# Reordering the opening of the two seven-product stages of a two-block transformer kernel

## The chip, the cores and the metric

One core of a Trainium2 chip. The metric is device time in microseconds (us); lower is better. Engines are named as in the profile: PE (TensorE matmul), PEld (its weight load), DVE (VectorE), ACT (ScalarE), POOL (GpSimd), SP (SyncE, which issues most loads).

## The reference, cut to what matters

All data are float32, 1024 tokens of width 1024. The first block (short convolution, stick-breaking attention) is untouched by the change. In the second block two wide projections matter here, each on a modulated norm `h` of the residual stream:

```python
h = _rmsnorm(x, norm1_g[l]) * (1.0 + scale1) + shift1
proj = h @ w_in[l]                    # 4352 columns: q, k, v of two attentions, two gates
...
h2 = _rmsnorm(x, norm2_g[l]) * (1.0 + scale2) + shift2
u = h2 @ w_up[l]                      # 2 x 2816 columns
a, g = jnp.split(u, 2, axis=-1)
a = ap[:, 0:s] * conv_w[0] + ap[:, 1:s + 1] * conv_w[1] + ap[:, 2:s + 2] * conv_w[2] + conv_b
x = x + gate2 * ((jax.nn.gelu(a, approximate=False) * g) @ w_down)
```

## The kernel before, in words

Channels lie on the 128 partitions, tokens along the free axis, in two halves of 512. Every fp32 product is made of three products of split operands (high by high, low by high, high by low), each part a rounded copy or the rest that it leaves. A high part is an ACT copy, a low part a DVE subtraction that waits for that copy.

Both projections run as two stages of one shape, called here the w_in stage (`U_IN2`, 15 blocks) and the w_up stage (`U_FFN`, 20 blocks). A stage opens with a `quad` (L1804): four ordinary units of 128 output columns, `q` to `q+3`, computed in the order (first pair, tokens 0 to 511), (second pair, both halves), (first pair, tokens 512 to 1023). Then come blocks `i` of 256 output columns, each by seven products (a Strassen-Winograd scheme, 2 by 2 by 2) of 12 matmuls of 128x128 by 128x512, in the order P1, P2, P6, P5, P7, P4, P3 (`sevens`, L1848). A block needs

- four weight sums on POOL (`weight_sums`, L1731), seven high parts on ACT (`weight_high`, L2274) and seven low parts on DVE (`weight_low`, L2966);
- three copies out of PSUM on ACT in the middle of the block (`snap`, L2305): snap 0 after P1, on which P6 waits; snap 1 after P6, on which P7 waits; snap 2 after P7, on which the first of four DVE `block_sum` (L2994) waits, and P3 waits on that one;
- for block 0 only, the sums of the tokens (`token_sums` L2984, 4 DVE subtractions for each of four chunks), their high parts on ACT (`token_high` L2296) and their low parts on DVE (`token_low` L2976), 16 of each.

What the blocks give is used further on. In the w_in stage `in2_copy` (L2325) takes a pair of the quad out of PSUM, `in2_use` (L2334) and `in2_low` (L3012) split a finished block of 128 columns into staging tiles, and `in2_store` (L2358) stores it by two DMAs of 512 KB, issued by ACT; the next use of a staging row waits until the store has landed. In the w_up stage each chunk `f` of 128 channels goes through a chain that changes engine at every step, for each half of the tokens: `first_tap` (ACT), `other_taps` (DVE, two instructions), `gelu` (ACT), the product with the gate (DVE; `first_product` for the two chunks of the quad, `gated` for others), `z_high` (ACT), `z_low` (DVE), and then `z_store` (two DMAs issued by ACT for both halves). One tile `yt` with two halves serves all chunks, so the next chunk's first tap in a half waits for the `z_low` of the chunk before it in that half.

Every engine executes its queue strictly in the order in which the program text issues it; nothing is reordered by a planner. The order inside a stage is written out by hand: `in2_act` (L2377) and the lines from L2544 for ACT, `in2_dve` (L3023) and the lines from L3152 for DVE. A semaphore wait holds back all that stands behind it on the same engine.

## Time and profile before

| what | value |
|---|---|
| median of 3 runs | 2747.52 us (2745.22 to 2749.78) |
| profiled execution, its own time | 2748.31 us |
| its span, first to last instruction | 2746.5 us |
| PE busy | 2600.3 us, 95% of the span |
| DVE, ACT, POOL busy | 56%, 40%, 31% |
| w_in stage, blocks 0 and 1 | from 1341.29 to 1387.04 us of the span |
| w_up stage, blocks 0 and 1 | from 2076.26 to 2136.50 us of the span |

The two openings are the stretches that the change is about; the rows below show them. In a timeline the idle time of an engine before a row stands in brackets, with the instruction that ended it.

### The profile page before, as it was taken

Reading aid. Unit: us, or ns where it says so; the run is one execution under the profiler, and the core shown is the slowest. Engines: PE = TensorE matmul, PEld = TensorE weight load, DVE = VectorE, ACT = ScalarE, POOL = GpSimd, SP = SyncE. Lnnn points to the kernel's source line nnn. Section 1 sums busy time; section 2 is a strip of 40 time slices with the busy share of each in tenths; the row PEclk is TensorE's granted clock in tenths of the full one; section 3 lists DMA queues with packets and bytes.
Section 4 is the critical chain, followed back from the end, with each engine's and each line's share of the span. In section 5 each row is a group of like instructions: output and inputs, shape, how many; then the busy total and the mean of one; then the engine's idle time right before and its main releaser. Section 6 shows DMA issues by size and latency. Waiting matters only on the chain.

```text
span 2746.5 us, 34710 instructions
## 1 busy us (share of the span) xinstructions
PE 2600.3 (95%) x12391; PEld 2162.4 (79%) x12391; DVE 1535.8 (56%) x2083; ACT 1109.9 (40%) x1865; POOL 855.9 (31%) x627
## 2 busy tenths in 40 slices
PE   6899999999899999999899998789997999999998
PEld 4788888788788799987688878668775888887887
DVE  5666665630324466657854437766578777771112
ACT  5201012511410688856543437661255555551000
POOL 2133331022233566620222220333101322325664
PEclk8999999999999999999999999999998999999999
DMA  6445443353365544435253346414242333339833
GB/s 226 127 125 149 131 149 98 89 191 113 124 211 163 130 108 108 108 127 160 88 183 122 108 138 171 159 33 169 79 136 91 100 117 108 108 109 304 285 93 122
DMA packets 377272, 374.81 MB, mean 136 GB/s; under 512 B 36323, under 2 KB 284556, under 8 KB 376972
## 3 DMA queue, kind: packets, MB, share of 16 engines
q1 hardware_dynamic: 346844, 303.91, 37.3%
q10 hardware_dynamic: 30256, 68.69, 6.7%
q8 instruction: 99, 1.62, 0.3%
q14 instruction: 73, 0.60, 0.1%
HBM read 286.55 MB, written 85.98 MB: 136 GB/s over the span
## 4 chain that ended last, share of the span: by engine, by line
PE 75%; DVE 12%; ACT 5%; DMA 3%; issue 2%; SPq 1%; POOL 1%; ACTq 0%; DVEq 0%; POOLq 0%
PE PS L1769 28%; PE PS L1857 20%; PE PS L1926 8%; PE PS L809 5%; PE PS L787 2%; PE PS L1816 1%; PE PS L1997 1%; DMA mod_raw<-in_w_ada 1%; PE PS L773 1%; PE PS L772 1%; DVE opBf L2991 1%; PE PS L1971 1%; ACT opA L2145 1%; PE PS L1839 1%; ACT opBf L2141 1%
## 5 line engine op out<-in xcount | busy, mean ns | idle before, releaser
L1769 PE MATMUL PS<-opA,w_hi 128*128 128x512 f32 x2176 | 680.3, 392 | 3.0 <-POOL w_lo L1575 3.0
L1769 PEld LDWEIGHTS PS<-opA,w_hi 128*128 128x128 f32 x2176 | 411.2, 189 | 89.0 <-POOL w_lo L1575 3.4
L1769 PE MATMUL PS<-opA,w_lo 128*128 128x512 f32 x1088 | 425.4, 391 | 0.0
L1570 POOL CAST w_hi<-w_raw 128x1024 fp32r<-128x1024 f32 (+1 forms) x117 | 121.3, 1037 | 795.7 <-PE PS L1769 467.3
L1857 PE MATMUL PS<-opB,Xr 128*128 128x512 f32 x1120 | 312.0, 396 | 17.4 <-ACT M L2321 17.4
L1575 POOL TENSOR_TENSOR w_lo<-w_raw,w_hi 128x1024 fp32r<-128x1024 f32 (+1 forms) x118 | 284.9, 2414 | 36.2 <-ACT w_hi L2200 26.8
L1857 PE MATMUL PS<-opA,Xr 128*128 128x512 f32 x980 | 277.3, 393 | 6.3 <-DVE M L3008 3.0
L1857 PEld LDWEIGHTS PS<-opB,Xr 128*128 128x128 f32 x1120 | 214.7, 192 | 64.1 <-ACT M L2321 18.6
L2656 DVE SCALAR_TENSOR_TENSOR M<-mod_raw,small,M 128x512 f32<-128x512 f32 x168 | 169.0, 1006 | 165.5 <-DMA mod_raw<-in_w_ada 88.6
L1769 PEld LDWEIGHTS PS<-opA,w_lo 128*128 128x128 f32 x1088 | 205.8, 189 | 42.7 <-issue 0.2
L1857 PEld LDWEIGHTS PS<-opA,Xr 128*128 128x128 f32 x980 | 183.0, 189 | 50.3 <-ACT M L2321 8.4
L2934 DVE SCALAR_TENSOR_TENSOR X<-PS,mod,X 128x512 f32<-128x512 f32 x64 | 48.1, 751 | 297.8 <-PE PS L1926 207.8
L1857 PE MATMUL PS<-opA,w_first 128*128 128x512 f32 x840 | 197.6, 391 | 5.6 <-ACT M L2331 5.6
L1857 PEld LDWEIGHTS PS<-opA,w_first 128*128 128x128 f32 x840 | 158.7, 189 | 39.0 <-ACT M L2331 6.0
L1743 POOL TENSOR_TENSOR X<-w_raw 128x512 f32<-128x512 f32 x36 | 48.5, 1347 | 379.6 <-DVE xn L2729 228.1
L1769 PE MATMUL PS<-opB,w_hi 128*128 128x512 f32 x512 | 159.9, 392 | 2.4 <-DVE opB L2922 1.4
L1128 DVE TENSOR_TENSOR_SCAN M<-PS,beta 128x896 f32<-128x896 f32 (+7 forms) x86 | 116.4, 1360 | 69.7 <-ACT PS L1004 61.8
L3008 DVE TENSOR_TENSOR M<-M,PS 128x512 f32<-128x512 f32 x140 | 96.3, 688 | 101.0 <-ACT M L2321 66.0
L2972 DVE TENSOR_TENSOR Xr<-X,Xr 128x512 fp32r<-128x512 f32 x140 | 117.0, 836 | 63.3 <-ACT Xr L2293 55.2
L1926 PE MATMUL PS<-opA,w_hi 128*128 128x512 f32 x480 | 149.2, 389 | 0.0
L2216 ACT ACTIVATE squares<-X 128x512 f32<-128x512 f32 x48 | 30.4, 633 | 232.6 <-DVE X L2934 229.2
L2321 ACT ACTIVATE M<-PS 128x512 f32<-128x512 f32 x105 | 62.8, 598 | 151.6 <-PE PS L1857 128.2
(266 smaller groups left out, 4794.9 us busy)
## 6 DMA issues: line engine op xcount, KB each, us to landing
mod_raw<-in_w_ada SPq DMA_DIRECT2D x96, 256.0 KB, 3.0
z_dram<-opB ACTq DMA_DIRECT2D x44, 512.0 KB, 3.9
w_raw<-in_a_w_in SPq DMA_DIRECT2D x32, 512.0 KB, 4.8
hin<-q_dram SPq DMA_DIRECT2D x64, 256.0 KB, 6.0
w_raw<-in_w_down SPq DMA_DIRECT2D x32, 512.0 KB, 3.9
opA<-z_dram SPq DMA_DIRECT2D x60, 256.0 KB, 5.3
mod_raw<-in_b_mod_w SPq DMA_DIRECT2D x48, 256.0 KB, 2.9
X<-x_dram SPq DMA_DIRECT2D x24, 512.0 KB, 6.9
```

The source lines that it names most:

```text
L787: ins = pe.transpose(PS[:, 4 + c % 2, (kb - NQ * p) * P:(kb - NQ * p + 1) * P], beta[n % BETAS][:, kb * P:(kb + 1) * P], ident[:])
L809: ins = pe.matmul(PS[:, o, q0 + cols_of.start:q0 + 2 * P], head_v[s][:, kb * P:(kb + 1) * P], a_T[i // 2][kb // NQ][:, kb % NQ, cols_of], ...
L1128: dve.tensor_tensor_scan(rest[n % FACTORS][:, 0:w][:, ::-1], stick_z(n)[:, ::-1], beta[n % BETAS][:, 0:w][:, ::-1], 1.0, ALU.mult, ALU.byp ...
L1570: pool.tensor_copy(hi, raw).then_inc(pool_done, 1)
L1575: pool.tensor_tensor(lo, raw, hi.bitcast(F32), ALU.subtract).then_inc(pool_done, 1)
L1769: ins = pe.matmul(ps, w[:, k0 + k, :], rhs(part, k0 + k), start=(k == 0 and n == 0), stop=(k == chunks - 1 and n == 2))
L1857: ins = pe.matmul(PS[:, seven_bank(i, which), :], seven_weight(q, i, which, w)[:, c * P:(c + 1) * P], token_part(which, part, c), start=(s ...
L1926: ins = pe.matmul(PS[:, down_bank(hf, n), :], w[:, s, k, :], z_operand(hf, g, part, k), start=(g == 0 and k == 0 and m == 0), stop=(g == 2 ...
L2321: act.activation(block_tile(q, i, 1)[:, 0:HALF] if n == 2 else M[1][:, n * HALF:(n + 1) * HALF], PS[:, seven_bank(i, P1), :], ACT.Copy).th ...
L2656: dve.scalar_tensor_tensor(out=acc, in0=mod_raw[:, n % 2, :], scalar=c, in1=acc, op0=ALU.mult, op1=ALU.add).then_inc(dve_done, 1)
L2972: dve.tensor_tensor(seven_weight(q, i, which, 1), seven_source(i, which), seven_weight(q, i, which, 0).bitcast(F32), ALU.subtract).then_in ...
L3008: dve.tensor_tensor(tile[:, hf * HALF:(hf + 1) * HALF], former, PS[:, seven_bank(i, which), :], ALU.add).then_inc(dve_done, 1)
```

## The change

On the order of work, in both stages:

- ACT's high parts: tokens of chunks 0 and 1, then the weights of P6, P5, P1 and P2, then the copies of the quad's second pair, and only then tokens of chunks 2 and 3 and the weights of P7 and P3. DVE follows with its low parts (P1 and P2 before the token sums of chunks 2 and 3).
- To free the P5 half of the PSUM early, the second of these copies goes aside: unit `q+3` is copied into a free half of `X` (chunks 6 and 7) by `in2_copy` in the w_in stage, and by the new `first_gates` in the w_up stage, where it is the gate of chunk 0.
- POOL's weight sums of block 1 wait for the last `token_low` of block 0.
- The high parts of the tokens of P7 and P4 wait for a new signal of PE in the middle of the quad's last quarter (`b12_read`), not for the end of unit `q+1`.
- Block 0's last two block sums move ahead of block 1's last weights on DVE; ACT's uses and stores of the quad's units take other places between block 1's weight copies.
- In the w_up stage chunk 0 is no longer finished first. Its copy goes into `M[4]` (`first_tile`), and its chain runs by halves: tokens 512 to 1023 inside block 1, tokens 0 to 511 from the end of block 1 into block 2. `copied_product` multiplies with the gate that was copied aside. Snap 0 of block 1 moves ahead of `gelu(2, 0)`.

The diff, cut to its core:

```diff
+        def z_former(f):
+            return {0: 2, 1: None, 2: None, 4: 0}.get(f, f - 2)
+        def gelu_former(f, hf):
+            return {1: None, 2: 1, 0: 2 if hf else 3, 4: 3 if hf else 0, 3: 0 if hf else 2}.get(f, f - 1)
+        def in2_halves(i, row):
+            return X[:, 6:8, HALF:T] if (i, row) == (-2, 1) else halves_of(block_tile(U_IN2, i, row)[:])
...
                     pool.wait_ge(seven_in[i % 2], at("seven_in", q, i))
+                    if i == 1:
+                        pool.wait_ge(dve_done, at("token_lo", q, P4, QK - 1))
...
+                        if (first, hf, k) == (0, 1, QK - 1):
+                            ins.then_inc(pe_done, 1)
+                            step(pe_done, "b12_read", u)
...
                 if which in (P7, P4):
-                    act.wait_ge(pe_done, at("unit", q + 1, 1))
+                    act.wait_ge(pe_done, at("b12_read", q))
...
                 weight_high(q, 0, P4)
-                token_high(q, P5, 0)
-                token_high(q, P6, 0)
+                for c in range(2):
+                    token_high(q, P5, c)
+                    token_high(q, P6, c)
                 weight_high(q, 0, P6)
                 weight_high(q, 0, P5)
-                token_high(q, P5, 1)
-                token_high(q, P6, 1)
-                weight_high(q, 0, P7)
-                weight_high(q, 0, P3)
-                for c in (2, 3):
-                    token_high(q, P5, c)
-                    token_high(q, P6, c)
                 weight_high(q, 0, P1)
                 weight_high(q, 0, P2)
                 for row in range(2):
                     in2_copy(-2, row)
+                for c in (2, 3):
+                    token_high(q, P5, c)
+                    token_high(q, P6, c)
+                weight_high(q, 0, P7)
+                weight_high(q, 0, P3)
                 for c in range(QK):
                     token_high(q, P7, c)
                 snap(q, 0, 0)
                 for c in range(QK):
                     token_high(q, P4, c)
+                weight_high(q, 1, P1)
+                snap(q, 0, 1)
+                weight_high(q, 1, P2)
                 for row in range(2):
                     in2_copy(-1, row)
-                snap(q, 0, 1)
-                for row in range(2):
-                    in2_use(-2, row)
-                weight_high(q, 1, P1)
-                weight_high(q, 1, P2)
-                for row in range(2):
-                    in2_store(-2, row)
+                in2_use(-2, 0)
                 snap(q, 0, 2)
+                in2_use(-2, 1)
                 weight_high(q, 1, P6)
                 weight_high(q, 1, P5)
                 for row in range(2):
+                    in2_store(-2, row)
+                weight_high(q, 1, P7)
+                for row in range(2):
                     in2_use(-1, row)
-                weight_high(q, 1, P7)
                 weight_high(q, 1, P4)
...
```

The same diff, ACT's order in the w_up stage from block 0's snap 2 on:

```diff
             for hf in range(2):
                 z_high(1, hf)
-            first_tap(2, 0)
             weight_high(q, 1, P7)
             weight_high(q, 1, P4)
+            first_tap(2, 0)
             z_store(1)
+            snap(q, 1, 0)
             gelu(2, 0)
             z_high(2, 0)
             first_tap(2, 1)
             for i in range(1, SEVENS[q]):
                 f = i + 2
-                snap(q, i, 0)
+                if i > 1:
+                    snap(q, i, 0)
                 weight_high(q, i + 1, P1)
                 weight_high(q, i, P3)
                 gelu(f - 1, 1)
                 z_high(f - 1, 1)
+                if i == 2:
+                    gelu(0, 0)
                 weight_high(q, i + 1, P2)
+                if i == 2:
+                    z_high(0, 0)
                 first_tap(f, 0)
                 z_store(f - 1)
+                if i == 2:
+                    z_store(0)
                 snap(q, i, 1)
                 weight_high(q, i + 1, P6)
                 gelu(f, 0)
+                if i == 1:
+                    first_tap(0, 1)
                 weight_high(q, i + 1, P5)
+                if i == 1:
+                    gelu(0, 1)
                 snap(q, i, 2)
                 weight_high(q, i + 1, P7)
                 weight_high(q, i + 1, P4)
                 z_high(f, 0)
+                if i == 1:
+                    z_high(0, 1)
                 first_tap(f, 1)
+                if i == 1:
+                    first_tap(0, 0)
...
```

DVE's order in the w_in stage behind the `token_low` instructions:

```diff
-                for row in range(2):
-                    in2_low(-2, row)
+                weight_low(q, 1, P1)
                 block_sum(q, 0, 1, 1)
+                weight_low(q, 1, P2)
+                in2_low(-2, 0)
                 block_sum(q, 0, 0, 0)
-                for which in (P1, P2, P6, P5):
-                    weight_low(q, 1, which)
+                weight_low(q, 1, P6)
+                weight_low(q, 1, P5)
+                in2_low(-2, 1)
+                block_sum(q, 0, 0, 1)
+                block_sum(q, 0, 1, 0)
+                weight_low(q, 1, P7)
                 for row in range(2):
                     in2_low(-1, row)
+                weight_low(q, 1, P4)
...
```

DVE's order in the blocks of the w_up stage from block 1 on:

```diff
+                other_taps(f - 1, 1)
+                weight_low(q, i + 1, P1)
+                weight_low(q, i, P3)
+                gated(f - 1, 1)
+                if i == 2:
+                    other_taps(0, 0)
+                block_sum(q, i, 0, 0)
+                z_low(f - 1, 1)
+                if i == 2:
+                    copied_product(0)
+                weight_low(q, i + 1, P2)
+                if i == 2:
+                    z_low(0, 0)
+                other_taps(f, 0)
+                weight_low(q, i + 1, P6)
+                weight_low(q, i + 1, P5)
+                if i == 1:
+                    other_taps(0, 1)
+                block_sum(q, i, 1, 1)
                 weight_low(q, i + 1, P7)
                 block_sum(q, i, 1, 0)
                 gated(f, 0)
+                if i == 1:
+                    copied_product(1)
                 weight_low(q, i + 1, P4)
                 z_low(f, 0)
+                if i == 1:
+                    z_low(0, 1)
                 block_sum(q, i, 0, 1)
```

## Rows read from the trace of the kernel before

**Rows 1.** The page's first part: busy time of each engine

```profile
PE 2600.3 (95%) x12391; PEld 2162.4 (79%) x12391; DVE 1535.8 (56%) x2083; ACT 1109.9 (40%) x1865; POOL 855.9 (31%) x627
```

**Rows 2.** Timeline of PE, w_in stage: start, duration, line, count, [idle before]

```profile
1324.68 11.04 PE L1816 MATMUL PS<-opA,opB 128*128 128x512 f32 x48
1341.29 7.16 PE L1857 MATMUL PS<-opA,w_first 128*128 128x512 f32 x24 [5.57 <-ACT M L2331]
...
1371.69 7.35 PE L1857 MATMUL PS<-opB,Xr 128*128 128x512 f32 x24 [2.34 <-ACT M L2321]
...
1387.04 5.60 PE L1857 MATMUL PS<-opA,w_first 128*128 128x512 f32 x24
```

**Rows 3.** Timeline of PE, w_up stage

```profile
2065.38 11.04 PE L1816 MATMUL PS<-opA,opB 128*128 128x512 f32 x48
2076.26 5.60 PE L1857 MATMUL PS<-opA,w_first 128*128 128x512 f32 x24
2085.59 7.08 PE L1857 MATMUL PS<-opB,Xr 128*128 128x512 f32 x24 [3.72 <-ACT M L2321]
...
2102.98 5.60 PE L1857 MATMUL PS<-opA,w_first 128*128 128x512 f32 x24
2119.91 8.59 PE L1857 MATMUL PS<-opB,Xr 128*128 128x512 f32 x24 [11.32 <-ACT M L2321]
...
2136.50 5.60 PE L1857 MATMUL PS<-opA,w_first 128*128 128x512 f32 x24
...
2155.54 5.60 PE L1857 MATMUL PS<-opA,w_first 128*128 128x512 f32 x24
```

**Rows 4.** Timeline of DVE, w_in stage

```profile
1323.01 2.87 DVE L2991 TENSOR_TENSOR opBf<-opBf 128x512 f32<-128x512 f32 x4
...
1332.91 5.76 DVE L2991 TENSOR_TENSOR opBf<-opBf 128x512 f32<-128x512 f32 x4
1339.38 1.49 DVE L2972 TENSOR_TENSOR w_first<-w_raw,w_first 128x512 fp32r<-128x512 f32 x2 [0.71 <-ACT w_first L2293]
1340.97 6.27 DVE L2980 TENSOR_TENSOR opB<-opBf,opB 128x512 fp32r<-128x512 f32 x8
...
1353.72 2.67 DVE L3019 SCALAR_TENSOR_TENSOR opB<-M,small,opB 128x1024 fp32r<-128x1024 f32 x2
...
1370.52 0.69 DVE L3008 TENSOR_TENSOR M<-M,PS 128x512 f32<-128x512 f32 x1
```

**Rows 5.** Timeline of ACT and its DMA queue, w_in stage

```profile
1355.77 3.51 ACTq L2367 DMA_DIRECT2D q_dram<-opB  x4
...
1363.09 1.15 ACT L2355 ACTIVATE opB<-M,small 128x1024 fp32r<-128x1024 f32 x1 [0.29 <-DMA q_dram<-opB]
...
1371.04 0.60 ACT L2321 ACTIVATE M<-PS 128x512 f32<-128x512 f32 x1 [5.31 <-DVE Xr L2972]
```

**Rows 6.** DMA issues, 1340 to 1430 us: count, size, median us to landing

```profile
q_dram<-opB ACTq DMA_DIRECT2D x16, 512.0 KB, 3.9
```

**Rows 7.** Timeline of POOL, w_in stage

```profile
1370.52 1.27 POOL L1743 TENSOR_TENSOR X<-w_raw 128x512 f32<-128x512 f32 x1 [2.01 <-DVE Xr L2972]
```

**Rows 8.** Timeline of ACT, w_up stage, block 2

```profile
2139.41 0.60 ACT L2321 ACTIVATE M<-PS 128x512 f32<-128x512 f32 x1 [0.45 <-PE PS L1857]
2144.81 1.19 ACTq L2529 DMA_DIRECT2D z_dram<-opB  x2
2146.13 0.60 ACT L2321 ACTIVATE M<-PS 128x512 f32<-128x512 f32 x1 [0.71 <-DVE w_first L2972]
```

**Rows 9.** Timeline of DVE, w_up stage, blocks 1 and 2

```profile
2108.31 2.37 DVE L3129 TENSOR_TENSOR opB<-yt,opB 128x512 fp32r<-128x512 f32 x2
2110.78 2.35 DVE L3140 SCALAR_TENSOR_TENSOR yt<-M,cols,yt 128x511 f32<-128x511 f32 x2
```

**Rows 10.** Windows: length, then busy us of PE, PEld, DVE, ACT, POOL; granted clock

```profile
2103.00:2136.50 33.50, 22.18 (x86) 17.74 (x84) 25.85 (x34) 15.60 (x24) 10.25 (x7) 0.80 0.28 95
...
2155.50:2174.60 19.10, 19.10 (x86) 15.79 (x86) 14.52 (x20) 10.23 (x17) 5.70 (x4) 1.00 0.35 111
```

More of the change, by code:

```diff
@@ L2330, in in2_copy @@
                 act.wait_ge(act_done, now(act_done))
-                act.activation(block_tile(U_IN2, i, row)[:], banks(bank(u, 0)), ACT.Copy).then_inc(act_done, 1)
+                if (i, row) == (-2, 1):
+                    act.wait_ge(x_half[1], at("x_half", U_IN2, 1))
+                act.activation(in2_halves(i, row), PS[:, bank(u, 0):bank(u, 0) + 2, :], ACT.Copy).then_inc(act_done, 1)
                 step(act_done, "in2_copy", u)
@@ L2354, in in2_use @@
                 else:
-                    act.activation(in2_stage(row, 0), halves_of(tile[:]), ACT.Copy, scale=in2_scale(in2_place(u))).then_inc(act_done, 1)
+                    act.activation(in2_stage(row, 0), in2_halves(i, row), ACT.Copy, scale=in2_scale(in2_place(u))).then_inc(act_done, 1)
                     step(act_done, "in2_used", u)
@@ L2498, in first_copies, with first_gates @@
                     act.wait_ge(pe_done, at("unit", u, 1))
-                    act.wait_ge(dve_done, at("fconv", f - 1, 1) if f else at("lo", "n2", 15))
+                    act.wait_ge(dve_done, at("lo", "n2", 15))
                     act.wait_ge(act_done, now(act_done))
-                    act.activation(M[0][:, hf * HALF:(hf + 1) * HALF], PS[:, bank(u, hf), :], ACT.Copy).then_inc(act_done, 1)
+                    act.activation(first_tile(f)[:, hf * HALF:(hf + 1) * HALF], PS[:, bank(u, hf), :], ACT.Copy).then_inc(act_done, 1)
                     step(act_done, "fa", f, hf)
                 names[("free", u)] = names[("fa", f, 1)]
+            def first_gates(u):
+                for hf in range(2):
+                    act.wait_ge(pe_done, at("unit", u, 1))
+                    act.wait_ge(x_half[1], at("x_half", U_FFN, 1))
+                    act.wait_ge(dve_done, at("lo", "n2", 15))
+                    act.wait_ge(act_done, now(act_done))
+                    act.activation(first_gate(hf), PS[:, bank(u, hf), :], ACT.Copy).then_inc(act_done, 1)
+                    step(act_done, "first_gate", hf)
             def gelu(f, hf):
@@ L2545, in _ @@
             weight_high(q, 0, P4)
-            token_high(q, P5, 0)
-            token_high(q, P6, 0)
+            for c in range(2):
+                token_high(q, P5, c)
+                token_high(q, P6, c)
             weight_high(q, 0, P6)
             weight_high(q, 0, P5)
-            token_high(q, P5, 1)
-            token_high(q, P6, 1)
-            weight_high(q, 0, P7)
-            weight_high(q, 0, P3)
+            weight_high(q, 0, P1)
+            weight_high(q, 0, P2)
+            first_copies(*CLASSIC[0])
+            first_gates(U_FFN + 3)
             for c in (2, 3):
@@ L2556, in _ @@
                 token_high(q, P6, c)
-            weight_high(q, 0, P1)
-            weight_high(q, 0, P2)
-            first_copies(*CLASSIC[0])
-            for hf in range(2):
-                first_tap(0, hf)
-            for hf in range(2):
-                gelu(0, hf)
+            weight_high(q, 0, P7)
+            weight_high(q, 0, P3)
             for c in range(QK):
@@ L2569, in _ @@
             first_copies(*CLASSIC[1])
-            snap(q, 0, 1)
-            for hf in range(2):
-                z_high(0, hf)
-            weight_high(q, 1, P1)
-            weight_high(q, 1, P2)
             for hf in range(2):
                 first_tap(1, hf)
-            z_store(0)
+            weight_high(q, 1, P1)
+            snap(q, 0, 1)
+            weight_high(q, 1, P2)
             snap(q, 0, 2)
@@ L2998, in block_sum @@
                 dve.wait_ge(act_done, at("snap", q, i, n))
-                if q == U_IN2:
+                if q == U_IN2 and (i, row) != (0, 1):
                     u = in2_unit(i - 2, row)
@@ L3123, in first_product, with copied_product @@
                 names[("free", u + 1)] = names[("fz", f, 1)]
+            def copied_product(hf):
+                dve.wait_ge(act_done, at("fg", 0, hf))
+                dve.wait_ge(act_done, at("first_gate", hf))
+                dve.wait_ge(dve_done, now(dve_done))
+                dve.tensor_tensor(yt[:, hf, :], yt[:, hf, :], first_gate(hf), ALU.mult).then_inc(dve_done, 1)
+                step(dve_done, "fz", 0, hf)
             def z_low(f, hf):
@@ L3157, in _ @@
             weight_low(q, 0, P5)
+            weight_low(q, 0, P1)
+            weight_low(q, 0, P2)
             token_sums(q, 2)
+            token_sums(q, 3)
             weight_low(q, 0, P7)
             weight_low(q, 0, P3)
-            token_sums(q, 3)
-            weight_low(q, 0, P1)
-            weight_low(q, 0, P2)
-            for hf in range(2):
-                other_taps(0, hf)
-            for c in range(QK):
-                token_low(q, P6, c)
-            for c in range(QK):
-                token_low(q, P5, c)
-            first_product(*CLASSIC[0])
-            for c in range(QK):
-                token_low(q, P7, c)
-            for c in range(QK):
-                token_low(q, P4, c)
-            for hf in range(2):
-                z_low(0, hf)
+            for which in (P6, P5, P7, P4):
+                for c in range(QK):
+                    token_low(q, which, c)
             weight_low(q, 1, P1)
+            weight_low(q, 1, P2)
             block_sum(q, 0, 1, 1)
@@ L3181, in _ @@
             block_sum(q, 0, 0, 0)
-            weight_low(q, 1, P2)
             first_product(*CLASSIC[1])
```

77 lines of the change are left out of this document (39 added, 38 removed).

## Prediction, made before the changed kernel had run

> **What bounds the kernel now.** I read the busy shares first: PE works 95% of the span, the next engine 56% [rows 1], so outside its gaps the time is PE's. Then PE's timeline in the two openings. A settled block of 84 matmuls takes 2155.54 - 2136.50 = 19.04 us [rows 3], 0.2267 us a matmul, 2.72 a product. In the w_in stage the quad's last 48 matmuls start at 1324.68 and could end at 1335.56; two blocks at full rate would bring block 2 to 1373.64, and it starts at 1387.04 [rows 2]: 13.4 us lost. In the w_up stage they could end at 2076.26, block 2 could start at 2114.34, and starts at 2136.50 [rows 3]: 22.2 us lost. Together 35.6 us, 1.3%, is the most that this change can give. The brackets name what PE waited for: in the w_in stage the copy of the quad (5.57 us, L2331) and snap 0 of block 1 (2.34); in the w_up stage snap 0 of blocks 0 and 1 (3.72, 11.32). All are ACT instructions at the end of a long queue, so the question is not whether PE waits but what stands ahead of each snap.
>
> The clock belongs to it. Behind the 11.32 us gap the granted clock of the window is 0.80 [rows 10], and the remaining 60 matmuls of the block take 2136.50 - 2119.91 = 16.59 us for 13.60: 3.0 us for the lower level. Behind 2.34 us of idle they take 15.35 (1.75 lost), behind 3.72 us 24 matmuls take 7.08 for 5.60 (1.5 lost) [rows 2, 3].
>
> I now walk the new queues by durations of rows. One 128x512 DVE subtraction takes 0.69 and follows the next at 0.72 to 0.80 us; 16 token lows take 2 x 6.27; `in2_low` 1.33 [rows 4]. Where POOL's sums run beside them, the four token sums of 2.87 take 5.76 [rows 4] and two z_low or two taps 2.4 instead of 1.5 [rows 9]: about 0.95 us of delay for each POOL sum. A block sum, which reads PSUM, keeps its 0.69 beside a running POOL sum [rows 4, 7].
>
> **W_in stage, block 0: the gain.** Copies of the quad now come before the last tokens, and POOL's four sums of block 1 no longer lie on the token sums, which take back their 2.87. From the second group of sums (end 1325.88): four weight lows behind their copies to 1329.74, eight token sums to 1335.5, two weight lows behind their ACT copies to 1337.8, then 16 lows at 0.784 to 1350.6, where before they ended at 1353.6. ACT has both copies done at 1331.1, so P1 starts at 1335.56 without the 5.57 us gap and its slow matmuls. The lows come each 3.14 us for a product of 2.72, so PE trails them: P6 1341.1, P5 1344.3, P7 1347.5, P4 1350.7, P3 1353.4, end 1356.1, against 1363.75: 7.6 us ahead. The early signal for P7 and P4 buys nothing here: their ACT copies are reached at 1337, after unit `q+1` anyway, and their lows wait in DVE's queue.
>
> **W_in stage, block 1: where it goes.** P6 of block 1 needs snap 0, and ACT reaches it only behind both stores of the units `q` and `q+1`. The chain ahead of it, from 1350.6: DVE does four weight lows, two block sums and two `in2_low` (7.5 us), and POOL's sums, moved to just here by the added wait, delay the ones that read SBUF twice by 4 x 0.95. So the second `in2_low` ends at 1361.9; before, both were done at 1356.39 [rows 4]. That is 5.5 us later, since its ACT copy now stands behind snap 2 and its DVE part behind two weight lows that wait for POOL. Then: store 1.2 (two DMAs), landing 3.9 us after the second issue at 1362.6 [rows 6], next use 1.15, `in2_low` 1.3 to 1.6, store 1.2, snap 0.6. Snap 0 ends at 1371.1 to 1371.9; I take 1371.5, against 1371.64 before [rows 5]. PE is idle from 1361.5 to 1371.5, ten microseconds; the nearest row is the 11.32 us gap, so the rest of the block takes 16.6 instead of 15.35, and block 2 starts at 1388.1 against 1387.04: **+1.1 us**. Bounds: with no POOL delay, and the clock loss of rows 2, -4; with the landing of rows 5 (the staging row was waited for until 1363.09, 3.8 us after the last issue had ended at 1359.28) and more delay by POOL, +3.
>
> **W_up stage, blocks 0 and 1.** The same walk: lows of P6 to P4 end at 2079.2, 2082.3, 2085.5 and 2088.7, because chunk 0's taps, gelus and product no longer stand among them. P6 starts at 2081.7, P7 at 2087.4 (ACT's second copies and first taps stand ahead of snap 1), and block 0 ends at 2095.6 against 2102.98: -7.4. P1 and P2 of block 1 end at 2101.0. Ahead of its snap 0 now stand chunk 1's whole chain, two weight copies, `first_tap(2, 0)` and `z_store(1)`: taps of chunk 1 beside POOL's sums to 2097.7, gelu, product to 2100.1, two weight lows, two block sums, `z_low` beside POOL 2103.4 to 2105.8 [rows 9], tap, store, snap 0 ended at 2107.8. P6 starts there, 12.1 us earlier than before. But the edit that moves snap 0 forward leaves `gelu(2, 0)`, `z_high(2, 0)` and `first_tap(2, 1)` between snap 0 and snap 1. From 2107.8: taps end 2110.3, product, z_high and tap 2113.5, two weight copies, gelu(2, 1) 2115.7, product, z_high 2118.1, tap and store, snap 1 ended at 2121.5. In a settled block it starts 6.72 us after snap 0 [rows 8]; here 13.7. PE has finished P5 at about 2115 and stands for 6 us; the clock falls again (1.6 us). Then `first_tap(0, 1)`, its taps and `gelu(0, 1)` stand ahead of snap 2, which P3 waits for by way of the block sum: it starts at 2130.2, 1.6 us late. Block 2 starts at 2133.0 against 2136.50: **-3.5 us**, bounds -6 and -1.
>
> **W_up stage, block 2.** In a settled block the queues have room as a whole: of 19.1 us DVE works 14.5, ACT 10.2 [rows 10]. But PE needs snap 1 10.9 us after the block's start, and it is there (2146.73 for 2147.38) 0.65 us before. That is all the cover there is, and everything inserted ahead of snap 1 beyond it is PE's time. Late already at the start: DVE's `copied_product(1)` and `z_low(0, 1)` and ACT's `z_high(0, 1)` and `first_tap(0, 0)` stand between block 1's end and snap 0, which starts at 2138.9, 5.9 us into the block instead of 2.9; P6 waits 1.1 us. Ahead of snap 1 come, in turns between engines, taps of (0, 0) on DVE to +5.4 us after snap 0 (+6.7 if POOL's sum goes first), gelu, block sum, z_low, `copied_product` +7.8, z_high +8.5, z_low +9.4, tap +10.3, and two stores of 1.19 each [rows 8] instead of one: snap 1 starts 12.1 to 13.4 us after snap 0, for 6.72. It ends at about 2152.4, PE wanted it at 2145.0, 7.4 us. Idle of that length lies between the 3.72 and 11.32 us rows; I take 2.0 for the clock. P7, P4 and P3 (8.16) end at 2162.6, block 3 started at 2155.54: **+7.1 us** for the stage, bounds +1 and +11. Behind it PE is the bound again and nothing gives time back; the later `z_store(0)` is read long after.
>
> **The sum.** 1.1 + 7.1 = 8.2 us. The profiled execution's 2748.31 (span 2746.5 and 1.8 around it) becomes 2756.5; it lies 0.8 above the median of 2747.52, so for a median 2755.7. Moving instructions without changing their size adds nothing else: the copy into `X` and the products with it have the shapes of before.
>
> Beside the 0.95 us the Trainium skill (SBUF, State Buffer, section Who interferes with whom) says that a VectorE instruction with two SBUF inputs and a GpSimd instruction that reads SBUF exclude each other for the whole instruction. The block sum of rows 4 and 7, undelayed, agrees. By that rule a loser would wait up to a whole sum; the rival "full delay" below prices it from rows.
>
> **Rivals.**
> - *Full delay by POOL* (10%): each DVE instruction that meets a sum waits for all its 1.27 us [rows 7], not 0.95. Three places (chain of w_in block 1, chains of w_up blocks 1 and 2) with 3 to 4 sums each on the path give 10 x 0.32 = 3.2 more: 2759. For it: z_low and taps at 2.4. Against: the 5.76 is an average over whole sums.
> - *Chunk 0's chain fits* (17%, the other side): the deferred half chains run while ACT would wait anyway, snap 1 of blocks 1 and 2 holds PE no more than before. Then block 2 starts at 2107.8 + 13.6 + 1.7 = 2123.1, block 3 at 2142 to 2144: -12; with +1.1 2736. For it: 4.6 us of idle DVE and 8.9 of ACT in a block [rows 10]. Against: the 0.65 us. It decides from where the two waits on snap 1 sum to less than about 3 us; between, the time is the next cases'.
> - *Block 1 of the w_in stage follows its block 0* (12%): the stores land and their uses go by 1362 or so; 7.6 stays, and with +7.1 the time is 2747.
> - *Same by halves* (11%): the walk is some 3 us too long in the w_up stage (each handover between engines rounded up): +3.5, 2751.
>
> **How the numbers follow.** What I walked has 50%, full delay 10%, and the others as given. The likeliest alone spans 2751 to 2761. A measurement here tells 0.2%, 5.5 us. Slower by more: 50 + 10 less 2 for the low end, 0.58; faster 0.17; the rest 0.25. The range takes the likeliest, full delay and the two cases near no change, and leaves out the fitting chain and the ends: 2745 to 2762.
>
> **What would show it.** PE's timeline: P1 of both stages without a gap; in the w_in stage one gap of about 10 us before P6 of block 1, block 2 at about 1388; in the w_up stage gaps of some 7, 6, 1.6, 1 and 7 us, all ended by snaps or the block sum, block 2 near 2133 and block 3 near 2162 (counted from the span's start, the later ones shifted by the w_in stage's change). ACT's row ahead of each late snap should be a store or tap that waited for DVE. Wrong it is if snap 1 of block 2 stands under 9 us behind snap 0, or if the second `in2_low` ends before 1358.

## The result, and the profile after

| | before | after |
|---|---|---|
| median of the runs made side by side | 2748.32 us (9) | 2753.34 us (9; 2750.65 to 2757.5) |
| ratio, 95% interval | | 1.0020 (1.0012 to 1.0029) |
| profiled execution: own time, span | 2748.31, 2746.5 us | 2750.65, 2748.9 us |
| span from the end of the w_in quad on | 1410.94 us | 1418.28 us |

The change costs 5.0 us, 3.3 to 8 by the interval. The last line needs a word: the stretch ahead of the w_in stage, to which no kernel here does anything, ends between 1330.62 and 1339.61 us in the profiled executions shown below. A difference of spans carries that scatter, so traces are compared from the quad's end (the start of P1 in the first PE rows below) on.

The page's first part, of the kernel after. Against [rows 1], PE is 2.0 us less busy in a span 2.4 longer: what was lost is waiting.

```profile
PE 2598.3 (95%) x12391; PEld 2160.6 (79%) x12391; DVE 1537.0 (56%) x2083; ACT 1110.8 (40%) x1867; POOL 856.3 (31%) x627
```

PE's timeline after, w_in stage, for [rows 2]:

```profile
1319.74 11.04 PE L1838 MATMUL PS<-opA,opB 128*128 128x512 f32 x48
1330.62 5.60 PE L1882 MATMUL PS<-opA,w_first 128*128 128x512 f32 x24
...
1351.31 5.60 PE L1882 MATMUL PS<-opA,w_first 128*128 128x512 f32 x24
1366.37 7.92 PE L1882 MATMUL PS<-opB,Xr 128*128 128x512 f32 x24 [9.46 <-ACT M L2350]
...
1382.51 5.60 PE L1882 MATMUL PS<-opA,w_first 128*128 128x512 f32 x24
```

P1 follows the quad with no gap, block 1 starts 20.69 us behind the quad's end for 28.19 before, and then one gap of 9.46 us takes all of it: block 2 starts at 51.89 for 51.48. The three smaller gaps of before (5.57, 1.57 and 2.34 us) became one large one.

PE's timeline after, w_up stage, for [rows 3]:

```profile
2071.51 5.60 PE L1882 MATMUL PS<-opA,w_first 128*128 128x512 f32 x24
...
2090.97 5.60 PE L1882 MATMUL PS<-opA,w_first 128*128 128x512 f32 x24
2103.45 8.02 PE L1882 MATMUL PS<-opB,Xr 128*128 128x512 f32 x24 [6.89 <-ACT M L2350]
2116.12 1.22 PE L1882 MATMUL PS<-opA,Xr 128*128 128x512 f32 x2 [4.64 <-ACT M L2350]
...
2125.77 3.01 PE L1882 MATMUL PS<-opA,Xr 128*128 128x512 f32 x12 [1.20 <-DVE M L3057]
2128.62 5.60 PE L1882 MATMUL PS<-opA,w_first 128*128 128x512 f32 x24
2135.05 5.78 PE L1882 MATMUL PS<-opB,Xr 128*128 128x512 f32 x24 [0.83 <-ACT M L2350]
2148.93 1.22 PE L1882 MATMUL PS<-opA,Xr 128*128 128x512 f32 x2 [8.11 <-ACT M L2350]
...
2158.97 5.60 PE L1882 MATMUL PS<-opA,w_first 128*128 128x512 f32 x24
```

Block 2 starts 57.11 us behind the quad's end (60.24 before: 3.1 won), block 3 at 87.46 (79.28 before: 8.2 lost). Block 2 takes 30.35 us, 11.3 more than a settled block, and 8.11 of it is one wait for snap 1.

What stands ahead of the two late snaps is in ACT's timeline. W_in stage, for [rows 5]; L2386 is `in2_use`, L2398 `in2_store`, L2350 the snap:

```profile
1350.43 7.11 ACTq L2398 DMA_DIRECT2D q_dram<-opB  x4
...
1360.83 1.15 ACT L2386 ACTIVATE opB<-M,small 128x1024 fp32r<-128x1024 f32 x1 [1.30 <-DMA q_dram<-opB]
...
1362.17 3.42 ACTq L2398 DMA_DIRECT2D q_dram<-opB  x4
1365.72 0.60 ACT L2350 ACTIVATE M<-PS 128x512 f32<-128x512 f32 x1 [3.00 <-issue]
```

W_up stage, block 2, for [rows 8]: snap 0, the stores of chunks 3 and 0, snap 1.

```profile
2134.40 0.60 ACT L2350 ACTIVATE M<-PS 128x512 f32<-128x512 f32 x1
...
2144.73 3.43 ACTq L2569 DMA_DIRECT2D z_dram<-opB  x4
2148.29 0.60 ACT L2350 ACTIVATE M<-PS 128x512 f32<-128x512 f32 x1 [2.82 <-issue]
```

Snap 1 starts 13.89 us behind snap 0, for 6.72 before. Both late snaps stand right behind four DMA issues, which hold the queue for 3.42 and 3.43 us; two hold it for 1.19 [rows 8]. (In the w_in stage four stood there before as well, at 1367.44, and held it for 3.48.)

DVE's timeline after, w_in stage, for [rows 4]:

```profile
1324.88 5.78 DVE L3040 TENSOR_TENSOR opBf<-opBf 128x512 f32<-128x512 f32 x8
...
1348.21 2.13 DVE L3068 SCALAR_TENSOR_TENSOR opB<-M,small,opB 128x1024 fp32r<-128x1024 f32 x1
...
1351.26 2.49 DVE L3021 TENSOR_TENSOR Xr<-X,Xr 128x512 fp32r<-128x512 f32 x2
1353.85 2.40 DVE L3068 SCALAR_TENSOR_TENSOR opB<-X,small,opB 128x1024 fp32r<-128x1024 f32 x1
...
1362.01 1.28 DVE L3068 SCALAR_TENSOR_TENSOR opB<-M,small,opB 128x1024 fp32r<-128x1024 f32 x1 [0.52 <-ACT opB L2386]
```

and POOL's, for [rows 7]: the first and the last of the four sums of block 1 that now wait for the token lows, and the first of block 2:

```profile
1345.73 1.82 POOL L1765 TENSOR_TENSOR X<-w_odd 128x512 f32<-128x512 f32 x1 [29.67 <-DVE opB L3029]
...
1351.66 1.53 POOL L1765 TENSOR_TENSOR X<-w_odd,X 128x512 f32<-128x512 f32 x1 [0.17 <-POOL X L1765]
1353.88 1.29 POOL L1765 TENSOR_TENSOR X<-w_raw 128x512 f32<-128x512 f32 x1 [0.69 <-DVE Xr L3021]
```

Eight token sums take 5.78 us, where the last four of them, beside POOL, had taken 5.76 [rows 4]; in exchange the two `in2_low` (1.28 in the last row) take 2.13 and 2.40, and the second ends 25.6 us behind the quad's end. The first is delayed by the sums that wait; the second starts at 1353.85, when these are done, and meets the first sums of block 2, the last row. In the w_up stage the same is seen on the taps and z_lows, for [rows 9]:

```profile
2099.03 2.43 DVE L3191 TENSOR_TENSOR opB<-yt,opB 128x512 fp32r<-128x512 f32 x2
...
2103.15 2.35 DVE L3202 SCALAR_TENSOR_TENSOR yt<-M,cols,yt 128x511 f32<-128x511 f32 x2
...
2120.02 3.54 DVE L3202 SCALAR_TENSOR_TENSOR yt<-M,cols,yt 128x512 f32<-128x512 f32 x2
```

The last are chunk 0's taps, beside two sums: 1.0 us of delay for each. The landing of a store is unchanged, for [rows 6]:

```profile
q_dram<-opB ACTq DMA_DIRECT2D x16, 512.0 KB, 3.9
```

Windows after, for [rows 10]: block 1 of the w_up stage, and a settled block.

```profile
2090.97:2128.62 37.65, 24.92 (x86) 19.13 (x84) 29.33 (x35) 17.09 (x27) 10.48 (x8) 0.82 0.28 85
...
2159.00:2178.10 19.10, 19.10 (x86) 15.83 (x85) 14.04 (x19) 10.28 (x16) 5.69 (x4) 1.00 0.35 111
```

DVE is busy 29.33 of block 1's 37.65 us, 78%, and ACT 45%: neither is full, and PE still stands 12.7 us. That points to the order; e7 below, which takes the half chain out of this block and puts its snaps forward, needs 27.76 us for it.

### The profile page after: what moved, and what is told of

It is laid out like the page before. It is cut to its first block, busy times and chain, and to the rows that moved or that the text cites. A ratio compares the mean times of both kernels' runs of the same rounds, so it can differ in the third digit from the quotient of the medians.

```text
span 2748.9 us, 34723 instructions
## 1 busy us (share of the span) xinstructions
PE 2598.3 (95%) x12391; PEld 2160.6 (79%) x12391; DVE 1537.0 (56%) x2083; ACT 1110.8 (40%) x1867; POOL 856.3 (31%) x627
## 4 chain that ended last, share of the span: by engine, by line
PE 76%; DVE 12%; ACT 4%; DMA 3%; issue 2%; SPq 1%; POOL 1%; ACTq 0%; DVEq 0%; POOLq 0%
PE PS L1791 29%; PE PS L1882 20%; PE PS L1953 8%; PE PS L829 5%; PE PS L1838 3%; PE PS L807 2%; PE PS L2024 1%; DMA mod_raw<-in_w_ada 1%; PE PS L793 1%; PE PS L792 1%; PE PS L1998 1%; DVE prob L1204 1%; PE PS L1864 1%; DVE yt L3202 1%; DVE Xr L3021 1%
## 5 line engine op out<-in xcount | busy, mean ns | idle before, releaser
L2705 DVE SCALAR_TENSOR_TENSOR M<-mod_raw,small,M 128x512 f32<-128x512 f32 x168 | 176.4, 1050 | 162.5 <-DMA mod_raw<-in_w_ada 83.4
L1882 PEld LDWEIGHTS PS<-opA,w_first 128*128 128x128 f32 x840 | 157.7, 188 | 32.7
L2350 ACT ACTIVATE M<-PS 128x512 f32<-128x512 f32 x105 | 62.8, 598 | 151.5 <-PE PS L1882 127.4
```

The source lines that it names most:

```text
L1882: ins = pe.matmul(PS[:, seven_bank(i, which), :], seven_weight(q, i, which, w)[:, c * P:(c + 1) * P], token_part(which, part, c), start=(s ...
L2350: act.activation(block_tile(q, i, 1)[:, 0:HALF] if n == 2 else M[1][:, n * HALF:(n + 1) * HALF], PS[:, seven_bank(i, P1), :], ACT.Copy).th ...
L2705: dve.scalar_tensor_tensor(out=acc, in0=mod_raw[:, n % 2, :], scalar=c, in1=acc, op0=ALU.mult, op1=ALU.add).then_inc(dve_done, 1)
```

## The experiments

All were timed in five rounds beside the kernel before. "Behind P1" is the span from the end of the w_in quad on, less that of before.

| run | us | less before | ratio, 95% interval | behind P1 |
|---|---|---|---|---|
| the change | 2753.34 | +5.0 | 1.0012 to 1.0029 | +7.3 |
| e1, w_in stage alone | 2748.17 | -0.3 | 0.9986 to 1.0003 | -1.1 |
| e2, w_up stage alone | 2755.47 | +7.0 | 1.0014 to 1.0036 | +9.9 |
| e3, half 0 behind snap 1 | 2752.24 | +3.8 | 1.0006 to 1.0024 | +5.9 |
| e4, snaps early in w_in block 1 | 2751.39 | +2.9 | 1.0004 to 1.0022 | +2.3 |
| e5, no wait on POOL | 2759.90 | +11.5 | 1.0033 to 1.0058 | +10.2 |
| e6, w_in alone, reordered | 2741.57 | -6.9 | 0.9964 to 0.9982 | -7.6 |
| e7, w_up alone, reordered | 2742.49 | -6.0 | 0.9973 to 0.9990 | -8.4 |
| e8, both reordered | 2734.84 | -13.6 | 0.9940 to 0.9965 | -17.3 |
| e9, second store behind snap 1 | 2754.86 | +7.4 | 1.0014 to 1.0032 | +4.7 |
| e10, before, snap 1 moved alone | 2739.40 | -8.1 | 0.9962 to 0.9984 | -10.9 |
| e11, e8 with five more moves | 2728.16 | -19.3 | 0.9912 to 0.9936 | -20.0 |
| e12, w_in of e11 with e10 | 2729.66 | -17.6 | 0.9922 to 0.9949 | -18.2 |

The last column and the times agree to within 3.7 us; smaller differences of one profile are not read as time.

**e1 and e2: one stage each.** The diff's hunks of the other stage are left as before, and the two shared edits are bound to one stage:

```diff
-                    if i == 1:
+                    if i == 1 and q == U_IN2:        # e1; U_FFN in e2
                         pool.wait_ge(dve_done, at("token_lo", q, P4, QK - 1))
```

> The change in the w_in stage alone; the w_up stage as before. Theory (the store chain ahead of snap 0 eats what block 0 gains): block 0 ends some 7.5 us earlier after the quad than before, P6 of block 1 follows a gap of 9 to 10 us, block 2 starts 51.9 us after the quad's end against 51.5, and the time is within 1.5 us of before. Rival (the w_in stage is faster and the w_up stage alone loses more than its trace shows): 2 to 4 us faster than before.

> The change in the w_up stage alone; the w_in stage as before. Theory: the whole loss is here, block 3 starts 87.5 us after the quad's end against 79.3, and the time is 6 to 8 us above before. Rival (the loss of the whole change comes from elsewhere, or is given back behind block 3): 0 to 3 us above before.

Measured -0.3 and +7.0, sum 6.7 for the whole change's 5.0. In e1's trace block 2 of the w_in stage starts at 51.86 behind one gap of 9.51 us; in e2's, block 3 of the w_up stage at 86.3, P7 of block 2 behind 8.15. So the loss is the w_up stage's, and the w_in stage gives back all that it gains.

**e3: chunk 0's half 0 behind snap 1.** Block 2 only:

```diff
+                if i == 2:
+                    gelu(0, 0)
+                    snap(q, i, 1)
                     z_high(0, 0)
                 first_tap(f, 0)
                 z_store(f - 1)
                 if i == 2:
                     z_store(0)
```

> The changed kernel with snap 1 of w_up block 2 issued ahead of z_high(0, 0), first_tap(4, 0) and both stores. Theory (what stands in ACT's queue ahead of snap 1 is PE's time): snap 1 starts about 7 us after snap 0 instead of 13.9, the gap of 8.1 us ahead of P7 of block 2 falls to under 2, P3 may wait 1 to 2 us for snap 2, and the time is 5 to 8 us below that of the changed kernel, at before or up to 3 us faster. Rival (the two engines' work in this block is simply too much, the wait moves to the next snap): the gap turns up ahead of P3 or of the next block's P6 with 5 us or more, and the time stays within 2 us of the changed kernel's, 3 to 5 us above before.

PE's timeline of e3, block 2:

```profile
2149.31 0.74 PE L1882 MATMUL PS<-opA,Xr 128*128 128x512 f32 x2 [1.18 <-ACT M L2350]
...
2159.33 4.62 PE L1882 MATMUL PS<-opA,Xr 128*128 128x512 f32 x12 [4.24 <-DVE M L3058]
```

The wait on snap 1 falls from 8.11 to 1.18, and 4.24 come back ahead of P3: the two stores now stand ahead of snap 2. Block 3 starts at 84.23 for 87.46, and of those 3.2 us the times show about one. Neither expectation came out whole: the wait went as the theory had it, the time did not (2752.24 beside 2753.34, intervals that overlap), and the rival had the gap ahead of P3, at 5 us or more. The edit also puts the next block's P2 copy ahead of `gelu(0, 0)`. Moving the snap ahead of the chain's end and the stores moves the wait.

**e4: snaps first in block 1 of the w_in stage.** ACT's order from `in2_store(-2, 0)` on, DVE's second block sum of the block, `block_sum(q, 1, 1, 1)`, ahead of `in2_low`:

```diff
+                snap(q, 1, 0)
                 weight_high(q, 1, P4)
+                in2_store(-2, 1)
+                in2_use(-1, 0)
+                snap(q, 1, 1)
+                in2_use(-1, 1)
...
+                snap(q, 1, 2)
+                in2_use(0, 0)
...
+                in2_use(0, 1)
```

> The changed kernel with snaps 0, 1 and 2 of w_in block 1 issued ahead of the uses and stores that wait for in2_low or for a landing, and its first block sum of PSUM's upper rows ahead of in2_low. Theory (ACT's queue order, not the amount of work or the POOL sums moved there, holds P6 for 9.5 us): P6 of block 1 waits under 3 us, block 2 starts 42 to 46 us after the quad's end against 51.9, some 2 to 4 us are lost again at block 2's snaps, and the time is 4 to 9 us below that of the changed kernel. Rival (DVE and the landings are the bound of this stretch): the gaps come back ahead of P7, P3 or block 2's P6, block 3 starts no more than 2 us earlier and the time is within 2 us of the changed kernel's.

The gap of 9.46 us is gone and block 2 starts at 40.22 for 51.89. But ACT then reaches `in2_use(0, 1)`, and all of block 2's snaps are behind it. ACT's timeline of e4:

```profile
1377.31 1.06 ACT L2386 ACTIVATE opB<-M 128x1024 fp32r<-128x1024 f32 x1 [4.24 <-DMA q_dram<-opB]
...
1379.31 3.43 ACTq L2398 DMA_DIRECT2D q_dram<-opB  x4
...
1384.35 0.60 ACT L2350 ACTIVATE M<-PS 128x512 f32<-128x512 f32 x1
```

PE waits 6.06 us for that snap, and block 3 starts at 67.95 for 70.93: 3.0 of 11.7 us kept. The time is 2.0 us below the changed kernel's, with intervals that overlap, where the theory wanted 4 to 9 and the rival at most 2: the queue order holds P6, as the theory said, but one block put in order passes most of the wait on to the next.

**e5: the wait on POOL taken out.**

```diff
-                    if i == 1:
-                        pool.wait_ge(dve_done, at("token_lo", q, P4, QK - 1))
```

> The changed kernel with one wait taken out: POOL's weight sums of block 1 no longer wait for the last token low of block 0 (both stages), so they run beside the token sums again, as in the kernel before. Theory (the wait moves POOL's collisions rather than removing them, and the late snaps are set by stores and landings): the third and fourth token sums take 5.8 us for 2.9, block 0 ends some 2 to 3 us later, the chain of block 1 is up to 3 us shorter; the time is within 2.5 us of the changed kernel's, 2750 to 2756. Rival (the moved sums are what makes the second in2_low and snap 0 of block 1 late): block 2 of the w_in stage starts 3 us or more earlier and the time falls to 2749 or less.

Both expectations failed: it is 6.6 us slower than the change. DVE's timeline of e5 in the w_in stage, eight token sums and eight token lows:

```profile
1331.11 7.72 DVE L3038 TENSOR_TENSOR opBf<-opBf 128x512 f32<-128x512 f32 x8
...
1341.14 8.04 DVE L3027 TENSOR_TENSOR opB<-opBf,opB 128x512 fp32r<-128x512 f32 x8
```

They take 5.78 and 6.27 where POOL is still, 0.9 to 1.0 less for each of the four sums beside them. P6 of block 0 waits 3.63 us for a low, block 1 starts at 24.51 for 20.69, and the chain behind it is no shorter, since `in2_low` meets the sums of block 2 (2.40). So the wait is worth having. Its worth in this trace is 2.9 us; that the times show 6.6, in five executions, stays unexplained.

**e6, e7, e8: other orders for what the change opened.** In the w_in stage the snaps of blocks 1 and 2 are put ahead of most of the uses and stores, which are spread and issued mostly one by one; snap 2 of block 2 still stands behind `in2_use(1, 1)` and a store. DVE's block sums follow. From block 2:

```diff
+                snap(q, 2, 0)
+                in2_use(0, 1)
+                weight_high(q, 3, P1)
+                weight_high(q, 2, P3)
+                in2_store(0, 1)
+                snap(q, 2, 1)
+                in2_use(1, 0)
```

In the w_up stage chunk 0's half chains go to blocks 4 and 6, stored by halves, and snap 1 goes ahead of the first tap and the store in every block from 2 on. In block 1 all three snaps and the second block sum go forward too, so that this run moves more than one thing:

```diff
+        CHUNK0 = {4: 1, 6: 0}
...
+                snap(q, i, 1)
                 first_tap(f, 0)
                 z_store(f - 1)
+                if i - 1 in CHUNK0:
+                    z_store_half(CHUNK0[i - 1])
                 weight_high(q, i + 1, P6)
                 gelu(f, 0)
+                if i in CHUNK0:
+                    first_tap(0, CHUNK0[i])
```

> The change in the w_in stage alone, with ACT's order of blocks 1 and 2 written so that every snap stands ahead of the uses and stores that wait for a landing. Theory (what the change lost in this stage is only the place of the snaps; PE keeps its 7.6 us of block 0 when no snap is queued behind a landing): block 3 starts 57 to 63 us behind the quad's end, against 70.5 before; 8 to 13 us faster than before, 2735 to 2740. Rival (the work must be done some time, and the waits reappear in blocks 3 and 4, as in the run with early snaps in block 1 alone): block 3 may start early, but the later blocks wait, and the time is 2743 or more.

> The change in the w_up stage alone, with chunk 0's two half chains moved to blocks 4 and 6 (in the half of yt that is free there) and stored by halves, and snap 1 of every block ahead of the first tap and the store. Theory (the queues of blocks 1 and 2 have no room for the chain, those of settled blocks have, once snap 1 doesn't stand behind it): block 2 starts 45 to 50 us behind the quad's end against 60.2 before, block 3 19 to 20 us later; 8 to 14 us faster than before, 2734 to 2740. Rival (each half chain costs PE the same wherever it stands, 4 to 7 us): blocks 4 and 6 take 23 us or more each for 19.2, and the time is 2743 or more.

> Both of these orders on the changed kernel. Theory (the two openings are apart and PE is the bound between them, so gains add): the sum of the two gains, 15 to 25 us faster than before, 2724 to 2733. Rival (they don't add, since something common, as the clock, gives part back): less than 0.8 of the sum of the two runs' gains.

PE's timeline of e8, w_in stage; its quad ends at 1336.62:

```profile
1357.26 5.60 PE L1894 MATMUL PS<-opA,w_first 128*128 128x512 f32 x24
...
1373.99 3.01 PE L1894 MATMUL PS<-opA,Xr 128*128 128x512 f32 x12 [0.25 <-DVE M L3110]
1376.84 5.60 PE L1894 MATMUL PS<-opA,w_first 128*128 128x512 f32 x24
...
1395.44 3.04 PE L1894 MATMUL PS<-opA,Xr 128*128 128x512 f32 x12 [2.11 <-DVE M L3110]
```

Here block 2 starts at 40.22, block 3 at 61.69 (in e6 at 63.35) for 70.52 before. No later block waits on account of it: e6's last block of the stage starts 7.1 us earlier than before's. The time of 2741.57 misses the theory's 2735 to 2740 by little, as block 3 misses its 57 to 63, and beats the rival's 2743. In the w_up stage both were half right: block 2 starts at 47.2, but block 3 follows 24.5 us later for the 19 to 20 expected, the time of 2742.49 lies between 2740 and 2743, and the blocks behind the half chains, 5 and 7, take 23.4 and 23.9 us for 19.04, so each half chain costs 4.4 to 4.9 us there too. The gains add: 6.9 + 6.0 = 12.9 for e8's 13.6, which rules out e8's rival; the 15 to 25 of its theory rested on larger gains of the two parts.

**e9: the second store alone.** `z_store(0)` moves from ahead of snap 1 of block 2 to behind it.

```diff
                 z_store(f - 1)
+                snap(q, i, 1)
                 if i == 2:
                     z_store(0)
-                snap(q, i, 1)
```

> The changed kernel, w_up block 2: z_store(0) issued behind snap 1 instead of ahead of it, nothing else moved. Theory (the two stores in a row held ACT's queue 3.43 us, where one holds it 1.19, and snap 1 of block 2 pays the difference): snap 1 comes 2.2 us nearer to snap 0 (11.7 us for 13.9), PE's wait ahead of P7 falls from 8.1 to about 5.9, and block 3 starts 2 us earlier, 85 to 85.7 us behind the quad's end for 87.5; the time falls by 1.5 to 2.5 us, 2750.5 to 2752. Rival (the chain of chunk 0 across the engines is what is late, and the wait only moves to snap 2 and P3, as in the run with half 0 behind snap 1): block 3 stays at 87 or later and the time within 1 us of the changed kernel's.

ACT's timeline of e9, block 2:

```profile
2149.68 1.19 ACTq L2569 DMA_DIRECT2D z_dram<-opB  x2
2151.00 0.60 ACT L2350 ACTIVATE M<-PS 128x512 f32<-128x512 f32 x1 [0.58 <-ACT yt L2580]
2151.08 2.03 ACTq L2569 DMA_DIRECT2D z_dram<-opB  x2
```

PE's wait ahead of P7 is 5.90 us, as the theory said; block 3 starts at 86.15, 1.3 earlier, between the two expectations; the time doesn't fall (2754.86 for 2753.34, intervals that overlap). The pair of issues behind the snap takes 2.03 us for 1.19, so that the two stores cost the queue 3.2 us in either place. The price of the term is shown by the wait, its worth in time is below what the runs tell.

**e10: snap 1 moved, and nothing else, in the kernel before.**

```diff
                 weight_high(q, i + 1, P2)
+                snap(q, i, 1)
                 first_tap(f, 0)
                 z_store(f - 1)
-                snap(q, i, 1)
```

> The kernel before, with one line moved: in the blocks of the w_up stage snap 1 stands ahead of the next chunk's first tap and of the store. Theory (the later blocks take 19.2 to 19.3 us for 19.04 because snap 1 is just too late in each): the blocks from 4 on take 19.04, some 15 of them gain 0.2 each, 2 to 3 us, and the time is 2745 to 2747 beside before's 2748.4. Rival (the 0.2 is the matmuls' own pace): no change in the blocks and the time within 0.7 us of before's.

8.1 us, three times what was expected. The settled blocks, 19.2 to 19.6 us long before, take 19.04, and the last block starts at 383.4 for 387.72 (4.3 us). The rest the expectation had overlooked: PE's timeline of the kernel before, in its last block,

```profile
2463.98 5.60 PE L1857 MATMUL PS<-opA,w_first 128*128 128x512 f32 x24
...
2477.58 1.21 PE L1857 MATMUL PS<-opA,Xr 128*128 128x512 f32 x2 [2.56 <-ACT M L2321]
```

shows 2.56 us of waiting for snap 1 and the slow matmuls behind (two in 1.21 us, for 0.62). e10 has no wait there, and its last block takes 19.05 us for 23.52 (from 2463.98 to the first matmul of the next stage at 2487.50): a wait of 2.56 cost 4.5. It repeats: from this block's start to the end of the span the nine profiled kernels that leave snap 1 in its place there take 281.05 to 282.52 us, the five that move it (e7, e8, e10, e11, e12) 276.80 to 277.64.

**e11: five more moves on e8**, one from each wait of its trace; the text of the expectation lists them. For instance:

```diff
-            for hf in range(2):
-                z_high(1, hf)
-            weight_high(q, 1, P7)
-            weight_high(q, 1, P4)
-            snap(q, 1, 0)
+            z_high(1, 0)
+            snap(q, 1, 0)
+            z_high(1, 1)
```

> The best version so far with five more moves, each from a wait that its trace showed. W_in stage: snap 2 of block 2 ahead of the last use (P3 waited 2.1). W_up stage: snap 0 of block 1 between the two z_high of chunk 1 (P6 waited 2.1); chunk 2's two halves side by side with snap 2 right behind (P3 waited 3.6); snap 0 of block 2 ahead of first_tap(3, 1) (P6 waited 4.3); behind the two blocks that carry a half chain of chunk 0, snap 1 ahead of z_high and the half store behind snap 2 (P7 waited 2.2 and 2.7, P3 1.6). Theory (each wait is a place in a queue, none is a lack of time on DVE or ACT): at least two thirds of these 18 us of waits and their slow matmuls go, the w_up stage's block 3 starts 60 to 64 us behind the quad's end for 71.7, blocks 5 and 7 take 19 to 20.5 for 23.4 and 23.9, and the time is 2717 to 2724 for 2734.8. Rival (DVE is the bound in the opening: its lows and chains pile up and the same time is waited for elsewhere): block 3 at 68 or later, time 2728 or more.

PE's timeline of e11, w_up stage; its quad ends at 2065.59:

```profile
2097.85 0.74 PE L1894 MATMUL PS<-opA,Xr 128*128 128x512 f32 x2 [1.43 <-ACT M L2362]
...
2105.81 4.58 PE L1894 MATMUL PS<-opA,Xr 128*128 128x512 f32 x12 [2.23 <-DVE Xr L3077]
...
2117.72 5.75 PE L1894 MATMUL PS<-opB,Xr 128*128 128x512 f32 x24 [1.86 <-ACT M L2362]
2127.47 1.22 PE L1894 MATMUL PS<-opA,Xr 128*128 128x512 f32 x2 [4.00 <-ACT M L2362]
```

The fastest of all, 2728.16, but not as fast as the theory had it. The w_in wait went, and block 5 fell from 23.4 to 21.2 us; block 7 still takes 23.1. In the w_up opening the rival won: block 2 starts at 44.65 instead of 46.07, block 3 at 73.06 instead of 71.66, and the waits stand elsewhere. DVE is busy 59.5 of those first 73.05 us.

**e12: the w_in stage of e11 with the w_up stage of e10.**

> The change in the w_in stage alone, with the reordered blocks 1 and 2 of the last version, and the w_up stage as in the kernel before with nothing but snap 1 ahead of the first tap and the store. Chunk 0 is finished first, as before. Theory (what the last version won in the w_up stage is the place of snap 1 in its settled blocks; the change's own w_up part, copying the gate aside and finishing chunk 0 by halves, gains nothing even in a better order): the gains of the two places add, 11 us in the w_in stage and 8 in the w_up stage, 2726 to 2730, the same as the last version's 2728.2 within 2.5 us; in the trace the last block of the w_up stage starts 383 to 384.5 us behind the quad's end, as in that version. Rival (the w_up part, once ordered well, is worth several microseconds): 2732 or more, and the last block at 388 or later.

2729.66, the same as e11 within the intervals; the last block of the w_up stage starts at 384.15. What e11 gains in the w_up stage is thus had by snap 1's place alone, a move of one line (e10 -8.1, e7 with it and the change's part -6.0); copying the gate aside and finishing chunk 0 by halves bring nothing in any of the orders tried.

## Why the prediction was right

It had slower by 8.2 us, 2755.7; measured are 8.6 in the two openings, 7.3 from the quad's end to the last instruction, and 2753.34, which is 5.0 slower. The direction and the mechanism came out as walked; the size came out in the trace, and in the times at three fifths. Point by point:

- **W_in stage, block 0.** As walked: P1 without a gap, block 1 at 20.69 for the 20.5 predicted (1356.1 - 1335.56). The lows set PE's pace through three waits of 0.2.
- **W_in stage, block 1.** One gap of 9.46 for "ten microseconds", P6 at 35.75 behind the quad's end for 35.94, by the chain named: second `in2_low`, store, landing, use, two stores, snap. Two terms were off and nearly cancelled: behind the last `in2_low` (ended 1363.29) the issues lasted 2.3 us more, not 1.2, and that `in2_low` ended 1.4 us earlier than walked (32.7 behind the quad's end for 34.1), half of it by the one before. Not all of the delay there is of the sums that the new wait moved: the second `in2_low` met one of block 2's. The stage lost 0.4 for the +1.1 forecast, inside its bounds: the slow stretch behind the gap took 16.14 for 16.6. e1 has it as no change.
- **W_up stage, blocks 0 and 1.** Gaps of 6.89, 4.64 and 1.20 for "7, 6, 1.6"; -3.1 for -3.5.
- **W_up stage, block 2.** The wait ahead of P7 was named with its cause, and was 8.11 for 7.4; snap 1 came 13.89 behind snap 0 for 12.1 to 13.4. The mis-sized term is "two stores of 1.19 each": 3.43 us. The stage lost 8.2 for 7.1. e9 shows the second store's share of the wait, 2.2 us, and e3 that the rest comes back ahead of P3 when the snap is moved; neither move takes it away.
- **What was not forecast.** The times show 5.0, not 8.6. Of the difference 1.3 is given back outside the openings in the trace; the other 2.3 lie within the scatter between profile and times and stay open. By the time alone, 5.0 would as well fit the case "same by halves" (3.5); it is block 3 at 87.46, 8.2 us late, that tells against it.
- **POOL's delays.** They are 0.85 to 1.1 us in each delayed row above, and 2.0 for the taps that met two sums: the estimate of 0.95 held, and the 1.27 of the rival "full delay" is not reached. The rule of the Trainium skill (SBUF, State Buffer, section Who interferes with whom), that a VectorE instruction with two SBUF inputs and a GpSimd instruction that reads SBUF contend, holds in direction: a block sum, which has one input in PSUM, keeps its 0.69 us beside a running sum (at 1350.47, beside the sum of 1349.43). That the loser always waits for the whole of the other is not what these averages show.
- **The rivals.** That chunk 0's chain fits is excluded by 8.11 us; that the w_in stage keeps its 7.6 us by 51.89. The second falls by the place of the snaps: e6 keeps the gain that the change itself gives back. The first does not fall by that alone: e3 moves the snap and gets about one microsecond, and in e7, e8 and e11 the half chains cost time where they are put.

## What to carry to other kernels

In a queue that never reorders, an early start upstream is worth nothing unless the instruction that the bounding engine needs next is issued ahead of everything that can wait; walk the queue from that instruction backwards, and do it for the two or three blocks that follow as well. Look for small waits of the bounding engine that repeat before the large ones of an opening: here 0.2 us in each of some fifteen blocks and 2.56 in the last were worth 8 us for one moved line. And follow a wait that is moved away to where it is next met before counting it as won.

## What the runs showed of the hardware

- DMA issues on ACT's queue cost more in a row: two take 1.19 us, four 3.42 and 3.43, and a second pair that starts 1.4 us behind the first takes 2.03 with a copy between them (e9).
- Behind a wait of 8.11 us two matmuls take 1.22 us for 0.62: PE is at the lower of its two levels, 1.2 for 2.4 GHz (the granted clock from 2148.93 to 2152.50 is 0.50), and over block 1 of the w_up stage the granted clock is 0.82 on average. Behind 2.56 us of idle in the last block of the kernel before it is 1.21 as well, and the slow matmuls add 1.9 us to the 2.56; behind 2.20 us in block 5 of e8 the two take 0.73. A short wait can cost most of its length again, and need not.
- The stretch ahead of the w_in stage, the same in all these kernels, differed by up to 9 us between their profiled executions (1330.62 to 1339.61), which is more than the change is worth. The times here are medians of five to eleven executions, and traces are compared from the quad's end on.
